# Softmax probabilities scaled on GpSimd: tensor_scalar in place of tensor_tensor with a broadcast operand

## The reference

```
s = einsum('bqhgd,bkhd->bhgqk', qi, k) * scale
p = softmax(s, axis=-1)
o = einsum('bhgqk,bkhd->bqhgd', p, v)
```

## Time and profile before

| | us |
|---|---|
| median of 3 runs | 1847.69 |
| lowest and highest | 1842.06, 1847.75 |
| the profiled execution | 1853.63 |
| its span, first to last instruction | 1851.8 |
| TensorE busy in it | 1742.4 |
| VectorE busy | 1185.2 |
| ScalarE busy | 864.6 |
| GpSimd busy | 585.8 |

### The profile page before, as it was taken

How to read it: one execution, slowest core, us unless ns; L and a number is a source line. 1 busy time by engine, 2 the same in 40 slices (tenths; PEclk the granted TensorE clock), 3 DMA queues, 4 the chain that set the end, 5 groups by cost and what they waited for, 6 DMA issues and landing times. The chain is left out here.

```text
span 1851.8 us, 29906 instructions
## 1 busy us (share of the span) xinstructions
PE 1742.4 (94%) x9859; PEld 1474.1 (80%) x9859; DVE 1185.2 (64%) x2379; ACT 864.6 (47%) x1860; POOL 585.8 (32%) x555
## 2 busy tenths in 40 slices
PE   7999999999899899899999999888999998999998
PEld 3777877777778778788888887777888777879997
DVE  5357588787677766567777663456564456756655
ACT  4566554444344443542222222556555454555543
POOL 0345443454444452111111000224335654321100
PEclk9999999999999999999999999889999999999999
DMA  8222333434334235244556654234343323446665
GB/s 294 63 67 66 75 93 91 104 112 119 105 86 103 81 69 165 86 130 146 149 157 209 217 186 70 70 83 96 88 119 103 98 75 81 126 137 182 184 201 158
DMA packets 344706, 224.10 MB, mean 121 GB/s; under 512 B 58038, under 2 KB 322540, under 8 KB 344556
## 3 DMA queue, kind: packets, MB, share of 16 engines
q1 hardware_dynamic: 335148, 215.88, 41.6%
q10 hardware_dynamic: 9408, 6.32, 1.3%
HBM read 221.06 MB, written 1.07 MB: 120 GB/s over the span
## 5 line engine op out<-in xcount | busy, mean ns | idle before, releaser
L2073 PE MATMUL bank<-Uhi,w_ring 128*128 128x512 f32 (+1 forms) x1536 | 549.5, 358 | 22.9 <-ACT H L1736 5.4
L2075 PE MATMUL bank<-Uhi,w_ring 128*128 128x512 f32 (+1 forms) x1536 | 533.5, 347 | 0.0
L2074 PE MATMUL bank<-Ulo,w_ring 128*128 128x512 f32 (+1 forms) x1536 | 533.5, 347 | 0.0
L1596 ACT ACTIVATE w_ring<-load_ring 128x512 fp32r<-128x512 f32 (+3 forms) x632 | 369.2, 607 | 151.5 <-PE bank L2075 111.7
L1817 DVE TENSOR_TENSOR w_ring<-load_ring,w_ring 128x512 fp32r<-128x512 f32 (+1 forms) x424 | 317.9, 766 | 171.8 <-ACT w_ring L1596 145.2
L2073 PEld LDWEIGHTS bank<-Uhi,w_ring 128*128 128x128 f32 x1536 | 296.0, 193 | 65.0 <-ACT H L1736 8.0
L2075 PEld LDWEIGHTS bank<-Uhi,w_ring 128*128 128x128 f32 x1536 | 295.8, 193 | 36.6
L1551 POOL TENSOR_TENSOR w_ring<-load_ring,w_ring 128x512 fp32r<-128x512 f32 (+3 forms) x208 | 247.7, 1197 | 239.2 <-ACT w_ring L1596 121.7
L2074 PEld LDWEIGHTS bank<-Ulo,w_ring 128*128 128x128 f32 x1536 | 296.2, 193 | 30.2
L1539 POOL TENSOR_TENSOR Y<-Y,small 128x512 f32<-128x512 f32 x160 | 172.1, 1076 | 299.2 <-DVE small L2017 284.8
L2022 DVE TENSOR_TENSOR Z<-bank,Z 128x512 fp32r<-128x512 f32 x160 | 109.9, 687 | 121.7 <-ACT Z L1721 120.3
(11 more groups left out here) (147 smaller groups left out, 2497.1 us busy)
## 6 DMA issues: line engine op xcount, KB each, us to landing
load_ring<-in_w_in SPq DMA_DIRECT2D x192, 256.0 KB, 2.9
load_ring<-in_w_ffn_in SPq DMA_DIRECT2D x160, 256.0 KB, 3.1
mod_ring<-in_w_mod SPq DMA_DIRECT2D x96, 256.0 KB, 3.3
load_ring<-in_w_ffn_out SPq DMA_DIRECT2D x88, 256.0 KB, 3.2
mod_place<-in_w_mod SPq DMA_DIRECT2D x64, 256.0 KB, 2.8
load_ring<-in_w_branch SPq DMA_DIRECT2D x48, 256.0 KB, 2.9
mod_w<-in_w_mod SPq DMA_DIRECT2D x16, 512.0 KB, 9.9
load_ring<-in_w_in SPq DMA_DIRECT2D x64, 128.0 KB, 2.5
```

The lines of the kernel that those rows point to most:

```text
L1596: act.activation(w_ring[:, plan.slot['w', key], 0, 0:sz], load_ring[:, plan.slot['load', key], 0:sz], ACT.Copy).then_inc(sem['w_hi'], 1)
L2073: pe.matmul(dst, lhs[0], rhs[0], start=start, stop=False)
L2074: pe.matmul(dst, lhs[0], rhs[1], start=False, stop=False)
L2075: return pe.matmul(dst, lhs[1], rhs[0], start=False, stop=stop)
```

## The change

In the GpSimd part of `den` the one `tensor_tensor` over the whole item, whose second operand is the reciprocal spread by a stride of zero over 512 columns (or 2 x 256), becomes one `tensor_scalar` for each column range of `subs(key)`, with the reciprocal as the scalar of each row. A latent item has one such instruction of 512 columns, a context item two of 256. The semaphore `prob_ready` is raised by the last. The instructions' places in the queue, the waits ahead of them and all other engines' instructions stay as they are; later lines of the file move up by two.

```diff
                     for name, k_ in plan.freed['Pn', key]:
                         pool.wait_ge(sem[name], count[name, k_])
-                    m = len(subs(key))
-                    w = NTOK // m
-                    pool.tensor_tensor(prob('Pn', key).rearrange("p (m k) -> p m k", m=m),
-                                       prob('P', key).rearrange("p (m k) -> p m k", m=m),
-                                       small[:, plan.slot['small', key], 10:10 + m].unsqueeze(2).to_broadcast([P, m, w]),
-                                       ALU.mult).then_inc(sem['prob_ready'], 1)
+                    for i, (a, b) in enumerate(subs(key)):
+                        ins = pool.tensor_scalar(prob('Pn', key)[:, a:b], prob('P', key)[:, a:b],
+                                                 small[:, plan.slot['small', key], 10 + i:11 + i], None, ALU.mult)
+                    ins.then_inc(sem['prob_ready'], 1)
```

## The result

The changed kernel takes 1863.16 us (median of 4 runs, 1858.9 to 1865.96) against 1847.48 us: the ratio is 1.009, with a 95% interval of 1.006 to 1.012. It is slower by about 16 us. The time lies above the range of the prediction (1841 to 1857), whose forecast was no measurable change.

A forecast was written before the change was run, and what follows sets the result against it. TensorE's work bounds the kernel, plus some 110 us of its waiting, all that GpSimd can reach. Rotary chain 1.4 plus transposes 0.5 gave 1.9 us off 1847.69: 1845.8 us, range 1841 to 1857.

The forecast's parts named there:

- The new instruction's cost: GpSimd's softmax multiply as tensor_scalar: 0.80 us for a latent item, 0.24 us less for each of 128.
- The upper end: Slowest case allowed for the new GpSimd form: a slower loop at twice the present time, 2.08 us.
- a multiply of two tensors, that of one with a broadcast, taken as one line: GpSimd multiply rows of 256 and 512 columns, read together as 1.5 ns a column over a fixed 0.27 us.
- the rate differs with the arithmetic: Reading of GpSimd's rows: subtraction 2.17 ns a column, multiply 1.5, so reading operands alone does not set the rate.
- The context pairs: 32 context items, each two instructions of 256 columns: 1.07 us together against 1.04; nothing counted as gained.
- The chain into the rotary embedding: Softmax multiply ahead of the rotary multiply, TensorE idle behind, at six places in layer 1: 6 x 0.24 = 1.4 us gained.
- rival 3: New form slower, at 2.08 us: 14.8 us lost, 1862.5 us; over 0.3% slower from a multiply of 1.57 us; chance 0.19.
- The transposes: Each item's four TensorE transposes need the multiply: some 0.5 us gained; 2.4 us lost if it is 0.53 us longer.
- VectorE's cover: A shorter GpSimd multiply is exposed a little less beside VectorE; counted at nothing, could go either way.
- The weight splits: Low halves of the weights, directly behind a multiply in 52 cases; counted at nothing, with 2.6 us as bound.
- Switching between kinds of instruction: GpSimd going between two instruction kinds: 0.13 us a change, 0.26 us an item, which only cancels the saving.
- The signs to look for: Multiply rows at 0.8 and 0.54 us; wrong if over 1.5 us, 0.5 or less, or TensorE's waits change elsewhere.

The follow-up runs named there:

- e9: Kernel before, with the slow one-operation tensor_scalar only at the 22 of 160 softmax multiplies directly ahead of a rotary multiply; ratio 1.0075, 13.9 us slower.
- e2: Kernel before, its softmax multiply kept as tensor_tensor but cut into three pieces (latent item) or four (context item); ratio 1.0079.
- e8: Kernel before, with the one-operation tensor_scalar in the second layer alone (64 latent items); ratio 1.0058, 10.7 us slower.
- e12: The changed kernel measured again without an edit, against the kernel before; ratio 1.0081.
- e10: Changed kernel, with the two-operation tensor_scalar at the 22 places ahead of a rotary multiply, one operation at the other 138; ratio 0.9998 against the kernel before.
- e3: Changed kernel, with the rotary multiply moved ahead of the softmax multiply where they are neighbours in GpSimd's queue; ratio 0.9982 against the kernel before.
- e4: Kernel before (tensor_tensor), with the rotary multiply moved ahead of the softmax multiply where they are neighbours in GpSimd's queue; ratio 0.9979.
- e6: Changed kernel, with a second operation (times 1.0) in every tensor_scalar; ratio 0.996 against the kernel before, 7.4 us faster.
- e7: Changed kernel with the second operation (times 1.0) and the rotary multiply ahead of its neighbouring softmax multiply; ratio 0.9938 against the kernel before, median 1837.26 us.
- e1: GpSimd instruction forms alone, whole computation left out; tensor_scalar of 512 columns took 1.562 us with one operation, 0.692 us with multiply then add.
- e5: More GpSimd forms alone, computation left out; at 512 columns multiply-multiply took 0.695 us, subtract-multiply and multiply-max 2.00, broadcast subtraction 1.040.
- e11: Kernel before, with two one-operation tensor_scalar of 256 columns for the 32 context items only; ratio 1.0009.

## Why so few places cost so much

In e9, 22 multiplies that are 0.51 us longer (1.584 against 1.079 us) could move TensorE by 22 x 0.51 = 11.1 us if every one were on the path in full:

```profile
L1548 POOL TENSOR_TENSOR Y<-Y,small 128x512 f32<-128x512 f32 x138 | 148.9, 1079 | 265.2 <-DVE small L2026 247.0 <-ACT w_ring L1605 7.5 <-PE bank L2084 5.7
L1542 POOL TENSOR_SCALAR Y<-Y,small 128x512 f32<-128x512 f32 x22 | 34.9, 1584 | 36.4 <-DVE small L2026 32.7 <-ACT w_ring L1605 3.7
```

They moved the time by 13.9. The interval (10.5 to 17.2) reaches down to 11.1, but in the traces something adds to the waits themselves: TensorE's clock. One of the chains has its rotary multiply at 1269.33 us in the kernel before:

```profile
1268.34 1.04 POOL L1539 TENSOR_TENSOR Y<-Y,small 128x512 f32<-128x512 f32 x1 [1.48 <-DVE small L2017]
...
1270.07 0.42 DVE L1960 TENSOR_TENSOR Y<-Y,tmp 96x256 f32<-96x256 f32 x1 [1.50 <-POOL Y L1524]
```

and in the kernel after:

```profile
1266.68 1.57 POOL L1538 TENSOR_SCALAR Y<-Y,small 128x512 f32<-128x512 f32 x1 [1.49 <-DVE small L2015]
...
1268.94 0.42 DVE L1958 TENSOR_TENSOR Y<-Y,tmp 96x256 f32<-96x256 f32 x1 [2.05 <-POOL Y L1524]
```

TensorE waits 1.58 us for this chain before and goes on at the full clock. In the kernel after it waits 2.15 us at the same matmul, and goes on at the lower one. The rows from there, before (granted clock after POOL's column) and after:

```profile
1271.30:1274.70 3.40, 3.40 (x27) 3.31 (x28) 1.84 (x5) 1.60 (x6) 0.46 (x1) 1.00 0.35 82
```

```profile
1270.30:1273.70 3.40, 3.40 (x17) 3.40 (x18) 1.39 (x4) 0.78 (x2) 0.46 (x1) 0.51 0.35 82
```

In 3.4 us TensorE ran 27 matmuls at 1.00 (2.4 GHz) and 17 at 0.51 (1.2 GHz for nearly all of it). Its timeline after the wait, in the kernel after:

```profile
1270.14 0.41 PE L2071 MATMUL bank<-Uhi,w_ring 128*128 128x256 f32 x1 [2.15 <-ACT H L1734]
1270.36 0.40 PE L2072 MATMUL bank<-Ulo,w_ring 128*128 128x256 f32 x1
1270.56 0.41 PE L2073 MATMUL bank<-Uhi,w_ring 128*128 128x256 f32 x1
```

and in the kernel before:

```profile
1271.27 0.39 PE L2073 MATMUL bank<-Uhi,w_ring 128*128 128x256 f32 x1 [1.58 <-ACT H L1736]
1271.49 0.28 PE L2074 MATMUL bank<-Ulo,w_ring 128*128 128x256 f32 x1
1271.61 0.28 PE L2075 MATMUL bank<-Uhi,w_ring 128*128 128x256 f32 x1
```

Matmuls start 0.21 us apart against 0.12. The twelve from here to the next `pv` take 2.55 us (1270.14 to 1272.69) against 1.54 (1271.27 to 1272.81): the 0.57 us longer wait cost 1.0 us more behind it. The other traces have the same matmul, and they fall into two groups: after waits of 1.89 to 2.16 us (after, e2, e8, e9, e12) the next 3.4 us had a mean granted clock of 0.53 to 0.62, after waits of 0.73 to 1.58 us (before and the six others) it was 1.00. The length of the wait doesn't settle it everywhere: at the chain whose TensorE wait ends at 1238.64 us, the kernel before waited 1.58 us too, and the next 3.4 us had 0.62.

Over the second layer's attention (1175 to 1620 us) TensorE's waits add up to 34.9 us before and 41.2 after, 6.3 of the 9.5 us; the lower clock stood for about 34 and 41 us in these stretches, which at half speed is some 3 us, the rest.

The same explains much of the spread between runs. The two profiled executions of the changed kernel are 7.9 us apart (spans 1858.7 and 1866.6 us), and (1 - mean granted clock) x span, the time that the lower clock would cost if TensorE never waited at it, is 39 us in the one and 49 in the other. Every run on record has its mean granted clock, so the same can be asked of all the runs behind the medians. Means over them, in us:

| kernel | runs | span | (1 - clock) x span | the rest |
|---|---|---|---|---|
| before, beside the next three | 23 | 1847.0 | 33.2 | 1813.8 |
| after, again (e12) | 6 | 1861.3 | 40.6 | 1820.7 |
| e9, 22 slow multiplies | 6 | 1860.4 | 40.9 | 1819.5 |
| e10, 138 slow, 22 fast | 12 | 1846.0 | 33.8 | 1812.2 |
| before, beside the next two | 23 | 1848.6 | 34.6 | 1814.0 |
| e3, slow, rotary first | 12 | 1844.7 | 33.2 | 1811.5 |
| e4, rotary first | 11 | 1845.0 | 30.0 | 1815.0 |
| before, beside the next two | 17 | 1846.8 | 33.5 | 1813.3 |
| e6, two operations | 12 | 1839.2 | 32.5 | 1806.7 |
| e7, both | 6 | 1834.7 | 30.3 | 1804.4 |

The changed kernel is 14.3 us longer than the one before, 7.4 of it in the clock's column and 6.9 in the rest; for e9 it is 13.4, with 7.7 and 5.7. The column is an upper value, as the lower clock costs nothing while TensorE waits: among the 23 runs of the kernel before in the first row, one microsecond more in it went with 0.7 us more of span. So, as an estimate from these runs, 5 to 7 us of the loss are the clock and 7 to 9 us direct waiting. The gain of e4 is all in the clock's column; that of e6 is nearly all in the rest.

## Why the prediction was wrong, point by point

- **The new instruction's cost: wrong, the first step that failed.** The prediction took 0.80 us, between half the streaming (0.65) and no change (1.04); it is 1.56 us alone and 1.60 in the kernel, twice that. The rows of before showed no tensor_scalar, and the premise that one tensor less means less time was an argument without a row. The upper end, 2.08 us, did contain the value. The point "a multiply of two tensors, that of one with a broadcast, taken as one line" was wrong as well, and so was the reading that the rate differs with the arithmetic. In e1 multiply and subtraction of two tensors both take 1.262 us; e5 shows that the broadcast operand itself saves 0.22 us, so the broadcast form was already the cheap one. Why line 1524, a multiply of two tensors of 256 columns, takes 0.65 us in the kernel when such a multiply takes 0.72 alone stays open.
- **The context pairs:** forecast 1.07 us, measured 1.87. That they cost next to nothing on the path was right (e11: 1.0009, interval up to 1.0022).
- **The chain into the rotary embedding: right in kind, mis-sized; the second step that failed.** The prediction counted six places, all in the second layer, those with TensorE idle directly behind in the timeline, at one us for one. There are 22 neighbours in the queue, 11 of them in the first layer, and e9 shows 13.9 us for them, 0.63 us for each. It named the chain of 1222 us, which grew by the 0.54 us of the multiply as said.
- **The price of a slower instruction, rival 3:** it put 5.5 us at a multiply of 1.57 us. The changed kernel is there and loses 14 to 16. So the wrong price alone would have left the time inside the range, whose upper end was reckoned for a multiply of 1.75 us. What took it out is the count of places (six for 22) together with the clock, for which no term stood in the sum and which is worth an estimated 5 to 7 us.
- **The transposes:** forecast 2.4 us for 0.53 us more. That sum took each gap in full as room, though its own least gap, 0.15 us, stands where TensorE waits; less 0.15 each, the 160 gaps lack 3.8 us. The waits that name the multiply grew by 3.9 us. But in e3, where they are 7.4 us against 1.3 in e4, the time is that of e4. Probably TensorE would have waited at the next point anyway; that is not shown.
- **VectorE's cover,** counted at nothing: its busy time grew by 5.3 us. What that did to the time can't be told apart here.
- **The weight splits:** counted at nothing, and right: 2.5 us against 2.6.
- **Switching between kinds of instruction,** taken at up to 0.13 us each from the earlier trace rows: nothing (e1).
- **The signs to look for** named over 1.5 us for the new form as what would make the prediction wrong; this is what happened.

## What to carry to other kernels

An elementwise instruction on GpSimd is priced by its exact form, not by its operand count; where the trace has no row for the form, a kernel of some fifty instructions measures it, and trying a second, neutral operation (times 1.0) can be worth a factor of two. In an in-order queue, look at what stands directly behind the instruction that is changed: 22 neighbours out of 160 carried nearly the whole loss, and swapping each pair gave 0.2% without touching the arithmetic. A half microsecond more of waiting can cost TensorE twice, once as waiting and once as a stretch at the lower clock; count the second from the granted clock of many runs, not from one profile.

## What was not expected of the hardware

- tensor_scalar on GpSimd, 128x512 in float32: 1.56 us with one operation, 0.695 us with multiply then multiply, 0.692 to 0.696 with multiply then add, 2.00 us with subtract then multiply or multiply then max. A copy takes 0.61 us. The Trainium skill, "GPSIMD Engine Reference", section "Engine selection", has one-input operations at roughly line-rate: 0.84 ns a column for the fast pair is one cycle of 1.2 GHz by that page's clock and agrees, 2.5 ns for the single operation is three and disagrees.
- A stride-zero operand makes tensor_tensor on GpSimd cheaper, 1.04 against 1.26 us, for the multiply and the subtraction alike.
- One wait of 2.15 us was followed by 3.4 us at a mean granted clock of about half, one of 1.58 us at the same matmul was not; at another matmul a wait of 1.58 us was.
